# Stage buffers of a two-block network start 128 bytes past a multiple of 512

## The chip, the cores and the metric

The kernel runs on one core of one Trainium2 chip. The metric is the device time of one launch, in microseconds (us), from the runs' own times; the profile is one further execution, taken by the hardware profiler.

## The reference

Two blocks of a network are applied in turn to 256 tokens of width 1024, all in float32. Cut to what matters:

```python
def swiglu(x, w_gu, w_down):
    gate, up = jnp.split(x @ w_gu, 2, axis=-1)
    return (jax.nn.silu(gate) * up) @ w_down          # 1024 -> 2 x 2816 -> 1024

def first_block(x, ...):
    for l in range(2):
        if l == 1: k, v = shared_kv(h, kv_norm_g, w_kv)
        h = h + 0.5 * rmsnorm(swiglu(rmsnorm(h, g[0]), ffn_w_gu[l, 0], ffn_w_down[l, 0]), g[1])
        mix = short_gated_conv(...) if l == 0 else diff_attention(...)
        h = h + rmsnorm(mix, g[3])
        h = h + 0.5 * rmsnorm(swiglu(rmsnorm(h, g[4]), ffn_w_gu[l, 1], ffn_w_down[l, 1]), g[5])

def second_block(x, ...):
    proj = rmsnorm_2(x, attn_norm) @ w_in              # q, k, v, index, SSD and gate columns
    y_attn = dsa_attention(...)                        # sparse attention over 64 chosen keys
    y_ssd = gated_group_rmsnorm(ssd_chunked(...), z, ssd_norm)
    merged = sigmoid(gate_a) * (y_attn @ w_attn_branch) + sigmoid(gate_b) * (y_ssd @ w_ssd_branch)
    x = x + merged @ w_out
    return x + hier_moe(rmsnorm_2(x, ffn_norm), ...)   # 32 experts, 2 of them for each token
```

## The kernel before

The program is one long sequence for each engine, written by hand, with semaphores between the engines. All weights but the experts' come as a stream of slots of 1 MB (128 partitions by 2048 floats). SP's queue loads slot after slot into `raw`, a ring of 6, as soon as TensorE has done with the slot 6 places before. ScalarE rounds each slot to the one-pass format fp32r (`whi`, line 318), VectorE takes the rest (`wlo`, line 329, which lies over `raw`), and the activations are split the same way into a high and a low part. Each product is then three matmuls: high by high, high by low, low by high.

Nearly all matmuls of the stream are of one kind: the stationary operand is a 128x128 piece of a split activation, loaded anew for each matmul, and the moving operand is 256 or 512 columns of `whi` or `wlo`. In the names of the profile `Y<-whi,hh` means: into `Y`, moving `whi`, stationary `hh`. Line 431 (`half_columns`) is gate and up of the feed-forward, with the normed input `xh`, `xl` as the stationary operand; line 461 (`some_rows`) is every product by a slot of rows, among them the down product with `hh`, `hl`; line 400 (`row_slot`) is the attention branch's product with `ya_hi`, `ya_lo`.

A feed-forward has 11 steps, each of 48 matmuls of line 431, the transposes of 256 hidden columns for two token tiles (line 728, moving `ident` in `cst`, stationary `hf`), and 24 matmuls of line 461. There are four feed-forwards. The other row products with a buffer of their own are the convolution's (`ch`, `cl`, 96 matmuls), the attention branch (`ya_hi`, `ya_lo`, 96) and the SSD branch (`ys_hi`, `ys_lo`, 192). Key and value, the attention output and the last product of block two use `xh` and `xl`.

The experts' weights are not split: their matmuls are plain fp32, with 32 gathered rows (`xt_rows`, line 2992, and `ht`, line 3013) stationary and 1 MB pieces in 20 places moving: the ring `raw`, the ring `whi` (named `raw_whi` there), `xh` and `xl` (named `raw_x`), `xn`, and `far`. SP's queue loads a piece when its place is free, first as the last slots of the stream are done with.

Where a buffer starts is set by the order of allocation. `align` puts a filler ahead of the buffers of a stage:

```python
        def align(name, where=ctx):
            short = -nc.sbuf_base % LINE          # LINE = 128
            if short:
                sb(name, [P, short // 4], where=where)
```

Every piece of a split activation that is loaded as a stationary operand starts a multiple of 512 bytes behind its buffer's start, and so does every 512-column piece of a weight slot. So one number tells how they lie: the start of the buffer modulo 512, called its residue here. Worked out from the allocations:

```
buffer                                   residue before   after
raw, wlo, whi, h, xn, xh, xl, cst             128           128
far                                           480           480
gains, gs, hf, hh, hl (feed-forward)          256           128
ch, cl, u, ut, bs (convolution)               256           128
kt, vt, qt, ex, at, qs, ov, on (attention)    256           128
tok_ya, ya_hi, ya_lo, zs, ys_lo, dd           256           128
xs, ys_hi, bt, ct, cb, mm, cr, no, one        256           128
vv, k2, qt2 (sparse attention)                256           128
adm, score, sm2, ex2                            0           384
xt_rows, ht_2, hf_2, gs_2, sel2 (experts)      64           480
gx (gathered rows)                             96             0
```

The small buffers `ss`, `rs` and `rt` (64 columns each) hold sums of squares, inverse roots and scratch. GpSimd computes the roots with a power of -0.5 that stands in a column of `rt`.

Of the kernel before, what the change touches and what calls it, by code (L numbers as in the profile page):

```python
# [8 lines left out]
ALU = mybir.AluOpType  # L9
ACT = mybir.ActivationFunctionType  # L10
X = mybir.AxisListType.X

P = 128
T = 256
NT = T // P
# [11 lines left out]
TILES = EXPERTS + EXTRA  # L27
PAIRS = TILES // 2
ABSENT = 4096
LINE = 128  # L30
NOWHERE = 1 << 20
PLACES = 20
EPS = 1e-6
# [88 lines left out]
def build(nc, stream, experts, x_in, out, cols, const, attn_const, adm_const, rows, lam_in, nothing):  # L122
# [7 lines left out]
    with ctx:  # L130
        def sb(name, shape, dt=F32, where=ctx):
            return where.enter_context(nc.sbuf_tensor(name, shape, dt))

        def align(name, where=ctx):

            short = -nc.sbuf_base % LINE
            if short:
                sb(name, [P, short // 4], where=where)

        def signal(name, base=0):  # L140
            return Signal(ctx.enter_context(nc.semaphore(name)), base)

        def pair(name):
            return [signal(f"{name}{t}") for t in range(NT)]
# [13 lines left out]
        col = sb("col", [P, N_COLS])  # L158
        ss = sb("ss", [P, 64])
        rs = sb("rs", [P, 64])  # L160
        rt = sb("rt", [P, 64])
        dt_raw = sb("dt_raw", [P, NT, 32])
        ident = cst[:, C_ID:C_ID + P]

# [39 lines left out]
        rstd_ready = pair("rstd_ready")  # L204
        yr_ready = pair("yr_ready")
# [33 lines left out]
        scratch_set = signal("scratch_set")  # L239
# [36 lines left out]
        plink = Link(ctx.enter_context(nc.semaphore("pool_order")))  # L276
# [226 lines left out]
        def rstd_of(t):  # L503
            return rs[:, 52 + t:53 + t]
# [29 lines left out]
        def pool_post_root(pool, t):  # L534

            a, y = ss[:, 50 + t:51 + t], rs[:, 50 + t:51 + t]
            pool.wait_ge(ysq_done[t].sem, ysq_done[t].at(1))
            plink(pool, nc.gpsimd.tensor_scalar(a, ss[:, 54 + 2 * t:55 + 2 * t], ss[:, 55 + 2 * t:56 + 2 * t], EPS,  # L538
                                                ALU.add, ALU.add))
            nc.gpsimd.tensor_tensor(y, a, rt[:, 63:64], ALU.pow).then_inc(yr_ready[t].sem, 1)  # L540

        def pool_rstd(pool, t):
            pool.wait_ge(hsq_done[t].sem, hsq_done[t].at(0))
            a = rt[:, 52 + t:53 + t]
            plink(pool, nc.gpsimd.tensor_scalar(a, ss[:, 52 + t:53 + t], EPS, None, ALU.add))
            nc.gpsimd.tensor_tensor(rstd_of(t), a, rt[:, 63:64], ALU.pow).then_inc(rstd_ready[t].sem, 1)

        def load_gain(i, after):
            @block.gpsimd
# [768 lines left out]
        class DiffAttention:  # L1318
# [34 lines left out]
            def run(self, kt, vt, scores_in, leave, then):  # L1353
# [4 lines left out]
                nm, su, rc, oq, og = self.nm, self.su, self.rc, self.oq, self.og  # L1358
# [208 lines left out]
                @block.gpsimd  # L1567
                def _(pool):
                    for t in range(NT):
                        pool_rstd(pool, t)  # L1570
                    for u in range(self.UNITS):
                        a = oq[:, u % 2, :]
                        pool.wait_ge(osq_done.sem, osq_done.at(u))
                        if u >= 2:
                            pool.wait_ge(on_ready.sem, on_ready.at(u - 2))
                        plink(pool, nc.gpsimd.tensor_scalar(a, a, EPS, None, ALU.add))
                        nc.gpsimd.tensor_tensor(og[:, u % 2, :], a, rt[:, 63:64].broadcast_to([P, 2]), ALU.pow
                                                ).then_inc(or_ready.sem, 1)
                    for t in range(NT):
                        leave.pool(pool, t)  # L1580
# [96 lines left out]
        def sparse_attention(tok_, ya_hi, ya_lo, iw, zs, dd, dsk, entry):  # L1677
# [20 lines left out]
            @block.gpsimd  # L1698
            def _(pool):
                for t in range(NT):  # L1700
                    pool.wait_ge(new_h[t].sem, new_h[t].base)
                pool.dma_start(adm[:, :, :], adm_const.rearrange("p (t k) -> p t k", t=NT)
                               ).then_inc(phase_in[1].sem, 16)
                pool.dma_start(gr[:, :, :], rows["qk"].partition_broadcast(P)).then_inc(phase_in[1].sem, 16)
                pool.dma_start(dsk[:, :, :], rows["ssd"].partition_broadcast(P)).then_inc(ssd_in.sem, 16)
# [53 lines left out]
            @block.gpsimd  # L1759
            def _(pool):  # L1760
                pool.wait_ge(key_squared.sem, NT)
                plink(pool, nc.gpsimd.tensor_scalar(rt[:, 40:42], ss[:, 40:42], EPS, None, ALU.add))
                nc.gpsimd.tensor_tensor(rs[:, 40:42], rt[:, 40:42], rt[:, 63:64].broadcast_to([P, 2]), ALU.pow
                                        ).then_inc(key_root.sem, 1)

            @block.tensor
# [185 lines left out]
            @block.gpsimd  # L1952
            def _(pool):

                g = nc.gpsimd
                x, m, e, z, z2, p, dt, da = (dd[:, i] for i in range(8))
                by_tile = [a.rearrange("p (t h) -> p t h", t=NT) for a in (x, dt, da)]
                pool.wait_ge(act_free.sem, act_free.at(2))
                pool.wait_ge(ssd_in.sem, 16)
                plink(pool, g.tensor_tensor(by_tile[0], dt_raw[:, :, :], dsk[:, 0:1, :].broadcast_to([P, NT, 32]), ALU.add))  # L1960
                plink(pool, g.tensor_scalar(m, x, 0.0, None, ALU.max))
                plink(pool, g.tensor_scalar(p, m, 2.0, None, ALU.mult))
                g.tensor_tensor(p, p, x, ALU.subtract).then_inc(dt_in.sem, 1)
                pool.wait_ge(dt_exp.sem, 2)
                plink(pool, g.tensor_scalar(z, e, 2.0, None, ALU.add))
                plink(pool, g.tensor_tensor(z, z, rt[:, 62:63].broadcast_to([P, NT * 32]), ALU.pow))
                plink(pool, g.tensor_tensor(z, z, e, ALU.mult))
                plink(pool, g.tensor_tensor(z2, z, z, ALU.mult))
                plink(pool, g.tensor_scalar(p, z2, 1.0 / 15, None, ALU.mult))
                for q in (13, 11, 9, 7, 5, 3):  # L1970
                    plink(pool, g.tensor_scalar(p, p, 1.0 / q, None, ALU.add))
                    plink(pool, g.tensor_tensor(p, p, z2, ALU.mult))
                plink(pool, g.tensor_scalar(p, p, 1.0, 2.0, ALU.add, ALU.mult))
                plink(pool, g.tensor_tensor(p, p, z, ALU.mult))
                plink(pool, g.tensor_tensor(dt, p, m, ALU.add))
                plink(pool, g.tensor_tensor(by_tile[2], by_tile[1], dsk[:, 1:2, :].broadcast_to([P, NT, 32]), ALU.mult))
                plink(pool, g.tensor_scalar(da, da, -1.0, None, ALU.mult))

                da4 = dd[:, 2:6].rearrange("p a b -> p (a b)").rearrange("p (t r h) -> p t r h", t=NT, r=4)
                for t in range(NT):  # L1980
                    g.tensor_copy(da4[:, t], by_tile[2][:, t, :].unsqueeze(1).broadcast_to([P, 4, 32])).then_inc(da_ready.sem, 1)
# [283 lines left out]
        class StateSpace:  # L2265
# [347 lines left out]
            def pool_root(self, pool, g):  # L2613
                a = ss[:, 2 * g:2 * g + 2]
                pool.wait_ge(gated_sq.sem, 2 * g + 2)
                plink(pool, nc.gpsimd.tensor_scalar(a, a, EPS, None, ALU.add))
                nc.gpsimd.tensor_tensor(rs[:, 2 * g:2 * g + 2], a, rt[:, 63:64].broadcast_to([P, 2]), ALU.pow
                                        ).then_inc(gated_root.sem, 1)

        place_far = (nc.sbuf_top - 5 * 4 * SLOT) // 32 * 32  # L2620
# [551 lines left out]
        @block.scalar  # L3172
        def _(act):
            act.wait_ge(scratch_set.sem, 1)
            nc.scalar.activation(rt[:, 60:61], rt[:, 61:62], ACT.Silu)
            act.wait_ge(cols_in.sem, 16)

        @block.vector
# [7 lines left out]
        class NormedEntry:  # L3186
# [8 lines left out]
                                     accum_out=ss[:, 52 + t:53 + t]).then_inc(hsq_done[t].sem, 1)  # L3195

            def root(self, pool, t):
                a = rt[:, 52 + t:53 + t]
                plink(pool, nc.gpsimd.tensor_scalar(a, ss[:, 52 + t:53 + t], EPS, None, ALU.add))
                nc.gpsimd.tensor_tensor(rstd_of(t), a, rt[:, 63:64], ALU.pow).then_inc(rstd_ready[t].sem, 1)  # L3200

            def scale(self, t):
                for c in range(2):
# [48 lines left out]

        @block.gpsimd
        def _(pool):
            nc.gpsimd.memset(rt[:, 60:62], 0.0).then_inc(scratch_set.sem, 1)
            plink(pool, nc.gpsimd.memset(rt[:, 63:64], -0.5))
            plink(pool, nc.gpsimd.memset(rt[:, 62:63], -1.0))

        first = ExitStack()
        align("rest_first", first)  # L3260
        gains = sb("gains", [P, 2, D], where=first)
        bufs = ffn_buffers(first, "_1")
# [33 lines left out]

        with ExitStack() as mixer:
            align("rest_ya", mixer)
            place_ya = (nc.sbuf_base + 31) // 32 * 32
            tok_ya = sb("tok_ya", [P, 4096], where=mixer)  # L3300
# [200 lines left out]
```

## Time and profile before

| what | value |
|---|---|
| median of 3 runs | 1675.75 us (1674.76 to 1676.12) |
| the profiled execution's own time | 1676.05 us |
| its span, first to last instruction | 1674.2 us |
| PE (TensorE matmul) busy | 1550.8 us, 93% of the span |
| DVE (VectorE) busy | 915.2 us |
| ACT (ScalarE) busy | 761.8 us |
| POOL (GpSimd) busy | 152.1 us |
| mean granted TensorE clock | 0.974 of 2.4 GHz |

The span is cut into stages in the order of the reference: the feed-forwards lie at about 9 to 200, 310 to 490, 541 to 720 and 828 to 1010 us, block two's projections and SSD at 1010 to 1350, its output products up to 1414, and the experts from there to the end. Matmuls overlap in the records: one of 512 columns is shown as lasting about 390 ns, while the next one starts about 230 ns after it. How fast TensorE works is read from the starts.

### The profile page before, as it was taken

To read this page: it belongs to the slowest core of one execution; us is meant where nothing else is said; L and a number is where in the kernel's file an instruction comes from. 1 tells how busy PE (TensorE), PEld (TensorE's weight loads), DVE (VectorE), ACT (ScalarE), POOL (GpSimd) and SP (SyncE) were. 2 spreads that over 40 slices of the span, in tenths; PEclk is the share of its full clock that TensorE was granted. 3 is DMA by queue.
4 is the path that set the end of the run, shared out by engine and by line. 5 is a ranking of instruction groups with operands and counts; after the bars stand their busy time and mean duration, and the time that the engine had idled before them with its cause. 6 is when DMAs were issued, how large, how long until landed. Compare 5 with 4: busy or idle time off the path is not lost.

```text
span 1674.2 us, 23054 instructions
## 1 busy us (share of the span) xinstructions
PE 1550.8 (93%) x9664; PEld 1253.5 (75%) x9664; DVE 915.2 (55%) x1298; ACT 761.8 (46%) x1201; POOL 152.1 (9%) x202
## 2 busy tenths in 40 slices
PE   7999999999999999997999999999999999677676
PEld 6888888788887888876788878877989977333332
DVE  5545576744564544577745455786866765410102
ACT  6444554544455444466644444547655653111111
POOL 0000000100010000011100001050001000232330
PEclk9999999999999999999999999999999999798998
DMA  7555555545557455532355554432452258999996
GB/s 280 187 179 195 204 164 176 188 177 186 191 176 281 162 178 191 184 126 102 139 194 183 183 194 139 170 109 101 173 176 102 102 186 337 354 415 414 413 415 271
DMA packets 55366, 347.23 MB, mean 207 GB/s; under 512 B 10516, under 2 KB 10916, under 8 KB 15168
## 3 DMA queue, kind: packets, MB, share of 16 engines
q1 hardware_dynamic: 47520, 333.17, 54.0%
q0 software_dynamic: 7744, 12.61, 2.3%
q8 instruction: 76, 1.25, 0.3%
q14 instruction: 26, 0.21, 0.0%
HBM read 396.34 MB, written 9.96 MB: 243 GB/s over the span
## 4 chain that ended last, share of the span: by engine, by line
PE 77%; DVE 7%; DMA 7%; ACT 4%; issue 3%; POOL 1%; DVEq 0%; SPq 0%; POOLq 0%; ACTq 0%
PE A L431 31%; PE Y L461 20%; PE A L384 6%; PE A L369 4%; PE A L2992 3%; DMA raw<-experts,extra 3%; PE Y L3013 2%; DMA raw_whi<-experts 2%; DVE wlo L329 1%; PE A L445 1%; PE Y L400 1%; DMA raw<-stream 1%; ACT whi L318 1%; PE A L728 1%; DVE xn L528 1%
## 5 line engine op out<-in xcount | busy, mean ns | idle before, releaser
L329 DVE TENSOR_TENSOR wlo<-raw,whi 128x2048 fp32r<-128x2048 f32 (+1 forms) x226 | 496.8, 2205 | 243.9 <-ACT whi L318 243.1
L318 ACT ACTIVATE whi<-raw 128x2048 fp32r<-128x2048 f32 (+1 forms) x226 | 415.6, 1847 | 91.2 <-DMA raw<-stream 91.1
L431 PE MATMUL A<-whi,xh 128*128 128x512 f32 x768 | 309.0, 402 | 5.1 <-DVE wlo L329 5.1
L431 PE MATMUL A<-whi,xl 128*128 128x512 f32 x768 | 301.9, 393 | 0.0
L431 PE MATMUL A<-wlo,xh 128*128 128x512 f32 x768 | 301.0, 392 | 0.0
L431 PEld LDWEIGHTS A<-whi,xh 128*128 128x128 f32 x768 | 145.1, 189 | 33.9 <-DVE wlo L329 5.9
L431 PEld LDWEIGHTS A<-whi,xl 128*128 128x128 f32 x768 | 145.0, 189 | 31.8
L431 PEld LDWEIGHTS A<-wlo,xh 128*128 128x128 f32 x768 | 145.5, 189 | 28.5
L461 PE MATMUL Y<-whi,hh 128*128 128x512 f32 x352 | 140.5, 399 | 1.2 <-DVE hl L808 1.2
L461 PE MATMUL Y<-whi,hl 128*128 128x512 f32 x352 | 138.9, 395 | 0.0
L461 PE MATMUL Y<-wlo,hh 128*128 128x512 f32 x352 | 138.9, 395 | 0.0
L770 ACT ACTIVATE hh<-A 128x256 fp32r<-128x256 f32 x88 | 33.9, 385 | 202.2 <-PE A L728 202.2
L384 PE MATMUL A<-whi,xh 128*128 128x256 f32 (+1 forms) x400 | 118.3, 296 | 4.7 <-DVE wlo L329 2.6
L384 PE MATMUL A<-whi,xl 128*128 128x256 f32 (+1 forms) x400 | 114.2, 285 | 0.0
L384 PE MATMUL A<-wlo,xh 128*128 128x256 f32 (+1 forms) x400 | 114.1, 285 | 0.0
L766 ACT ACTIVATE gs<-A,rs 128x256 f32<-128x256 f32 x88 | 41.8, 475 | 135.8 <-PE A L431 135.8
L808 DVE TENSOR_TENSOR hl<-A,hh 128x256 fp32r<-128x256 f32 x88 | 37.0, 420 | 98.5 <-ACT hh L770 97.6
L538 POOL TENSOR_SCALAR ss<-ss 128x1 f32<-128x1 f32 x12 | 13.0, 1084 | 852.3 <-ACT xn L513 852.3
L3083 DVE TENSOR_TENSOR xt_rows<-A,col 128x512 f32<-128x512 f32 x24 | 16.6, 691 | 134.8 <-PE A L2982 134.8
L384 PEld LDWEIGHTS A<-whi,xh 128*128 128x128 f32 x400 | 77.7, 194 | 10.0 <-issue 7.6
L816 DVE SCALAR_TENSOR_TENSOR hf<-A,rs,gs 128x256 f32<-128x256 f32 x88 | 42.4, 482 | 69.6 <-ACT gs L766 69.5
L2992 PE MATMUL A<-far,xt_rows 128*32 128x256 f32 x432 | 53.4, 462 | 28.2 <-DMA raw<-experts,extra 24.8
(464 smaller groups left out, 2798.3 us busy)
## 6 DMA issues: line engine op xcount, KB each, us to landing
raw<-stream SPq DMA_DIRECT2D x216, 1024.0 KB, 4.8
raw_whi<-experts SPq DMA_DIRECT2D x39, 1024.0 KB, 28.5
raw<-experts SPq DMA_DIRECT2D x22, 1024.0 KB, 28.0
far<-experts SPq DMA_DIRECT2D x17, 1024.0 KB, 26.5
raw_x<-experts SPq DMA_DIRECT2D x12, 1024.0 KB, 28.9
xn<-experts SPq DMA_DIRECT2D x6, 1024.0 KB, 28.1
gains<-post_rows POOLq DMA_DIRECT2D x6, 512.0 KB, 5.2
far<-sums_at SPq DMA_DIRECT2D x4, 512.0 KB, 8.3
```

Of the source, the lines that this page charges most:

```text
L318: nc.scalar.activation(whi[:, n % RING, c], raw[:, n % RING, c], ACT.Copy).then_inc(hi_ready.sem, 1)
L329: nc.vector.tensor_tensor(wlo[:, n % RING, c], raw[:, n % RING, c], whi[:, n % RING, c].bitcast(F32), ALU.subtract).then_inc(lo_ready.sem, 1)
L369: ins = nc.tensor.matmul(bank[:, m, :], lhsT=lhs, rhs=rhs, start=(k == 0 and q == 0), stop=(k == KD - 1 and q == 2))
L384: ins = nc.tensor.matmul(bank[:, m, :], lhsT=lhs[:, k, tok(m)], rhs=w[:, k, 0:width], start=(k == 0 and q == 0), stop=(k == KD - 1 and q = ...
L431: ins = nc.tensor.matmul(bank, lhsT=lhs[:, kk, tok(t)], rhs=w[:, k, :], start=(kk == 0 and q == 0), stop=(kk == KD - 1 and q == 2))
L461: ins = nc.tensor.matmul(banks[c], lhsT=lhs[:, j, :], rhs=w[:, j, cc], start=(start and j == 0 and q == 0), stop=(stop and j == 1 and q == 2))
L766: nc.scalar.activation(gs[:, t, s % 2, :], bank(t, s)[:, 0:256], ACT.Silu, scale=rstd_of(t)).then_inc(gate_ready[t].sem, 1)
L770: nc.scalar.activation(hh[:, t, turns % 2], bank(t, turns)[:, 0:256].rearrange("p (j t) -> p j t", j=2), ACT.Copy).then_inc(hid_hi[t].sem, 1)
L808: v_.tensor_tensor(hl[:, t, s % 2], bank(t, s)[:, 0:256].rearrange("p (j t) -> p j t", j=2), hh[:, t, s % 2].bitcast(F32), ALU.subtract).t ...
L816: v_.scalar_tensor_tensor(hf[:, t, s % 2, :], bank(t, s)[:, 256:512], rstd_of(t), gs[:, t, s % 2, :], ALU.mult, ALU.mult).then_inc(hid_rea ...
L2992: ins = nc.tensor.matmul(gate_up(q)[group(c, j), :], lhsT=xt[:, q % 2, k, group(part, j)], rhs=w[j][:, k, c, :], start=(part == 0 and k == 0),
L3013: ins = nc.tensor.matmul(down_bank(q)[group(c, j), :], lhsT=ht[:, q % 2, group(f, j)], rhs=w[j][:, f, c, :], start=f == 0, stop=f == 1)
```

## The change

The filler of `align` now brings the next buffer to 128 modulo 512 bytes, where before it brought it to a multiple of 128. `rt` is cut from 64 to 40 columns, and the columns of it that GpSimd and one warm-up activation used move to free columns of `ss`. No buffer before `dt_raw` moves, and the residues of all others are in the table above. The instructions of every engine, their order, their shapes and their waits are the same as before; a few read or write `ss` where they had `rt`.

```diff
-LINE = 128
+LINE, LINE_START = 512, 128
...
         def align(name, where=ctx):
 
-            short = -nc.sbuf_base % LINE
+            short = (LINE_START - (nc.sbuf_base + 31) // 32 * 32) % LINE
             if short:
                 sb(name, [P, short // 4], where=where)
...
-        rt = sb("rt", [P, 64])
+        rt = sb("rt", [P, 40])
...
         def pool_rstd(pool, t):
             pool.wait_ge(hsq_done[t].sem, hsq_done[t].at(0))
-            a = rt[:, 52 + t:53 + t]
+            a = ss[:, 58 + t:59 + t]
             plink(pool, nc.gpsimd.tensor_scalar(a, ss[:, 52 + t:53 + t], EPS, None, ALU.add))
-            nc.gpsimd.tensor_tensor(rstd_of(t), a, rt[:, 63:64], ALU.pow).then_inc(rstd_ready[t].sem, 1)
+            nc.gpsimd.tensor_tensor(rstd_of(t), a, ss[:, 63:64], ALU.pow).then_inc(rstd_ready[t].sem, 1)
...
-            nc.gpsimd.memset(rt[:, 60:62], 0.0).then_inc(scratch_set.sem, 1)
-            plink(pool, nc.gpsimd.memset(rt[:, 63:64], -0.5))
-            plink(pool, nc.gpsimd.memset(rt[:, 62:63], -1.0))
+            nc.gpsimd.memset(ss[:, 60:62], 0.0).then_inc(scratch_set.sem, 1)
+            plink(pool, nc.gpsimd.memset(ss[:, 63:64], -0.5))
+            plink(pool, nc.gpsimd.memset(ss[:, 62:63], -1.0))
```

## Rows read from the trace of the kernel before

**Rows 1.** The page: span, and busy time of each engine.
```profile
span 1674.2 us, 23054 instructions
...
PE 1550.8 (93%) x9664; PEld 1253.5 (75%) x9664; DVE 915.2 (55%) x1298; ACT 761.8 (46%) x1201; POOL 152.1 (9%) x202
```

**Rows 2.** Windows 60-200, 320-495, 550-720, 840-1000 us, in the feed-forwards: their sum.
```profile
sum 645.00, PE 644.59 PEld 525.76 DVE 328.10 ACT 283.62 POOL 7.21; mean PE 161.15 PEld 131.44 DVE 82.02 ACT 70.90 POOL 1.80
```

**Rows 3.** The chain that ended last, one step of a feed-forward: start, us, what.
```profile
75.91 5.48 PE A L431 x24
81.38 5.59 PE Y L461 x24
```

**Rows 4.** Groups on PE: busy us, mean ns of one; out<-moving,stationary.
```profile
L461 PE MATMUL Y<-whi,hh 128*128 128x512 f32 x352 | 140.5, 399 | 1.2 <-DVE hl L808 1.2
...
L461 PE MATMUL Y<-whi,ys_hi 128*128 128x512 f32 x64 | 25.6, 400 | 1.5 <-DVE wlo L329 1.5
...
L461 PE MATMUL Y<-whi,ch 128*128 128x512 f32 x32 | 13.0, 407 | 0.7 <-DVE cl L1113 0.7
...
L400 PE MATMUL Y<-whi,ya_hi 128*128 128x512 f32 x32 | 10.1, 397 | 0.0
```

**Rows 5.** Timeline of PE: starts with a stationary operand at residue 128.
```profile
60.14 0.39 PE L431 MATMUL A<-whi,xh 128*128 128x512 f32 x1
...
63.99 0.40 PE L431 MATMUL A<-whi,xl 128*128 128x512 f32 x1
...
523.92 0.39 PE L461 MATMUL Y<-whi,xl 128*128 128x512 f32 x1
...
532.08 0.39 PE L461 MATMUL Y<-whi,xl 128*128 128x512 f32 x1
```

**Rows 6.** Timeline of PE: starts with a stationary operand at residue 256.
```profile
64.23 0.40 PE L461 MATMUL Y<-whi,hh 128*128 128x512 f32 x1
...
69.58 0.40 PE L461 MATMUL Y<-whi,hl 128*128 128x512 f32 x1
...
1233.29 0.62 PE L400 MATMUL Y<-whi,ya_lo 128*128 128x512 f32 x2
...
1254.21 0.62 PE L400 MATMUL Y<-whi,ya_lo 128*128 128x512 f32 x2
...
1367.21 0.40 PE L461 MATMUL Y<-whi,ys_hi 128*128 128x512 f32 x1
...
1372.81 0.40 PE L461 MATMUL Y<-whi,ys_hi 128*128 128x512 f32 x1
```

**Rows 7.** Timeline of PE: residue 128 behind residue 256, and behind transposes.
```profile
355.88 0.39 PE L431 MATMUL A<-whi,xh 128*128 128x512 f32 x1
...
358.39 0.39 PE L431 MATMUL A<-whi,xl 128*128 128x512 f32 x1
...
538.39 0.39 PE L461 MATMUL Y<-wlo,xh 128*128 128x512 f32 x1
...
540.70 0.39 PE L461 MATMUL Y<-whi,xl 128*128 128x512 f32 x1
```

**Rows 8.** Tile xt_rows: the expert stage's fp32 matmuls, ns min/median/max.
```profile
L2992 PE MATMUL A<-raw,xt_rows x480: 379/379/636, 1448.5 to 1649.7; 128*32 128x256 f32 x160
...
L2992 PE MATMUL A<-far,xt_rows x432: 376/379/636, 1441.8 to 1656.0; 128*32 128x256 f32 x144
```

**Rows 9.** Windows of the end: us, PE, PEld, DVE, ACT, POOL, PEclk, DMA share, GB/s.
```profile
1441.00:1551.00 110.00, 88.83 (x1084) 44.29 (x1088) 16.12 (x36) 15.64 (x37) 32.51 (x32) 0.89 0.98 391
1551.00:1650.00 99.00, 67.83 (x823) 32.98 (x815) 9.38 (x18) 12.11 (x30) 26.53 (x27) 0.90 1.00 408
```

**Rows 10.** The chain around the start of the expert stage.
```profile
1350.26 36.71 PE Y L461 x156
...
1459.43 10.88 DMA raw<-experts,extra
```

**Rows 11.** Timeline of SP's queue: expert loads wait for stream slots.
```profile
1390.65 1.28 SPq L2666 DMA_DIRECT2D far<-experts  x3
```

More of the change, by code:

```diff
@@ L539, in pool_post_root @@
                                                 ALU.add, ALU.add))
-            nc.gpsimd.tensor_tensor(y, a, rt[:, 63:64], ALU.pow).then_inc(yr_ready[t].sem, 1)
+            nc.gpsimd.tensor_tensor(y, a, ss[:, 63:64], ALU.pow).then_inc(yr_ready[t].sem, 1)
         def pool_rstd(pool, t):
             pool.wait_ge(hsq_done[t].sem, hsq_done[t].at(0))
-            a = rt[:, 52 + t:53 + t]
+            a = ss[:, 58 + t:59 + t]
             plink(pool, nc.gpsimd.tensor_scalar(a, ss[:, 52 + t:53 + t], EPS, None, ALU.add))
-            nc.gpsimd.tensor_tensor(rstd_of(t), a, rt[:, 63:64], ALU.pow).then_inc(rstd_ready[t].sem, 1)
+            nc.gpsimd.tensor_tensor(rstd_of(t), a, ss[:, 63:64], ALU.pow).then_inc(rstd_ready[t].sem, 1)
         def load_gain(i, after):
@@ L1576, in _ @@
                         plink(pool, nc.gpsimd.tensor_scalar(a, a, EPS, None, ALU.add))
-                        nc.gpsimd.tensor_tensor(og[:, u % 2, :], a, rt[:, 63:64].broadcast_to([P, 2]), ALU.pow
+                        nc.gpsimd.tensor_tensor(og[:, u % 2, :], a, ss[:, 63:64].broadcast_to([P, 2]), ALU.pow
                                                 ).then_inc(or_ready.sem, 1)
@@ L1761, in _ @@
                 pool.wait_ge(key_squared.sem, NT)
-                plink(pool, nc.gpsimd.tensor_scalar(rt[:, 40:42], ss[:, 40:42], EPS, None, ALU.add))
-                nc.gpsimd.tensor_tensor(rs[:, 40:42], rt[:, 40:42], rt[:, 63:64].broadcast_to([P, 2]), ALU.pow
+                plink(pool, nc.gpsimd.tensor_scalar(ss[:, 44:46], ss[:, 40:42], EPS, None, ALU.add))
+                nc.gpsimd.tensor_tensor(rs[:, 40:42], ss[:, 44:46], ss[:, 63:64].broadcast_to([P, 2]), ALU.pow
                                         ).then_inc(key_root.sem, 1)
@@ L1965, in _ @@
                 plink(pool, g.tensor_scalar(z, e, 2.0, None, ALU.add))
-                plink(pool, g.tensor_tensor(z, z, rt[:, 62:63].broadcast_to([P, NT * 32]), ALU.pow))
+                plink(pool, g.tensor_tensor(z, z, ss[:, 62:63].broadcast_to([P, NT * 32]), ALU.pow))
                 plink(pool, g.tensor_tensor(z, z, e, ALU.mult))
@@ L2616, in pool_root @@
                 plink(pool, nc.gpsimd.tensor_scalar(a, a, EPS, None, ALU.add))
-                nc.gpsimd.tensor_tensor(rs[:, 2 * g:2 * g + 2], a, rt[:, 63:64].broadcast_to([P, 2]), ALU.pow
+                nc.gpsimd.tensor_tensor(rs[:, 2 * g:2 * g + 2], a, ss[:, 63:64].broadcast_to([P, 2]), ALU.pow
                                         ).then_inc(gated_root.sem, 1)
@@ L3174, in _ @@
             act.wait_ge(scratch_set.sem, 1)
-            nc.scalar.activation(rt[:, 60:61], rt[:, 61:62], ACT.Silu)
+            nc.scalar.activation(ss[:, 60:61], ss[:, 61:62], ACT.Silu)
             act.wait_ge(cols_in.sem, 16)
@@ L3197, in root @@
             def root(self, pool, t):
-                a = rt[:, 52 + t:53 + t]
+                a = ss[:, 58 + t:59 + t]
                 plink(pool, nc.gpsimd.tensor_scalar(a, ss[:, 52 + t:53 + t], EPS, None, ALU.add))
-                nc.gpsimd.tensor_tensor(rstd_of(t), a, rt[:, 63:64], ALU.pow).then_inc(rstd_ready[t].sem, 1)
+                nc.gpsimd.tensor_tensor(rstd_of(t), a, ss[:, 63:64], ALU.pow).then_inc(rstd_ready[t].sem, 1)
             def scale(self, t):
```

## The prediction

> **What bounds the kernel now.** The page comes first: PE is busy for 1550.8 of 1674.2 us, DVE and ACT for 915 and 762 [rows 1]. Then the windows, since a share over the whole span says little: in four stretches inside the feed-forwards, 645 us together, PE is busy for 644.6 us [rows 2]. No other engine comes near, so a nanosecond off a matmul there is a nanosecond off the time. The chain of waits agrees: one step of a feed-forward is a chain of PE pieces alone [rows 3].
>
> A busy PE is not a fast PE, because matmuls overlap in the records. The mean durations of the groups, some 400 ns, can't be added up [rows 4]. What counts is the distance from one start to the next. I looked at it for one shape, 512 columns moving, a fresh 128x128 stationary piece for each matmul, moving operand always in `whi` or `wlo` (residue 128). The reader is to compare two groups:
>
> - Stationary piece at residue 128. Line 431 with `xh`, `xl` starts at 60.14 and, 17 starts later, at 63.99 us: 226.5 ns each. Line 461 with `xh`, `xl` (key and value) goes from 523.92 to 532.08 us in 36 starts: 226.7 ns [rows 5].
> - Stationary piece at residue 256. Line 461 with `hh`, `hl` goes from 64.23 to 69.58 us in 23 starts: 232.6 ns. Line 400 with `ya_hi`, `ya_lo` needs 20.92 us for 90 starts: 232.4 ns. Line 461 with `ys_hi`, `ys_lo` needs 5.60 us for 24: 233.3 ns [rows 6].
>
> So one line of code, 461, runs at 226.7 or at 232.6 ns by which buffer is stationary. The layout inside the buffer doesn't explain it: `ya_hi` and `ys_hi` are laid out as `xh` is, pieces 1024 bytes apart, and are as slow as `hh`, whose pieces are 512 bytes apart. Nor do the neighbours: the two stretches at 60 to 70 us stand in the same feed-forward, one right behind the other. What is left is where the buffer lies, and the residue is the part of that which all the buffers at 232 to 233 ns share.
>
> **The change part by part.**
>
> *Row products with a stage buffer.* `hh`, `hl`, `ch`, `cl`, `ya` and `ys` go from residue 256 to 128, where `xh` is. Their number: three passes each of 352 with `hh`, 64 with `ys_hi`, 32 with `ch` and 32 with `ya_hi` [rows 4], so 3 x 480 = 1440 matmuls. Each is to lose 232.6 - 226.7 = 5.9 ns [rows 5, 6]. 1440 x 5.9 ns = 8.5 us. The bounds: 0 if place above some address is the cause and not the residue; for the other end, the fastest pace of rows 5 against the slowest of rows 6, 6.8 ns, 9.8 us.
>
> *What follows them.* A block of line 431 behind a block with `hh` opens slower than it goes on: 11 starts in 2.51 us, 228.2 ns, from 355.88 us [rows 7]. Against 226.7 that is 16 ns for a block, and 48 such blocks stand in the timeline: 0.8 us. I take it, because a block at one residue throughout should have nothing to settle. The bounds are 0 and 0.8.
>
> *What the transposes leave.* Behind a group of transposes the pace is 231.0 ns for ten starts, 2.31 us from 538.39 us, although both operands of the matmuls are at residue 128, and the transposed `h` and `cst` too [rows 7]. That is 43 ns lost for each block behind transposes, and the change doesn't touch its cause. Twenty of the blocks to be sped up open that way (counted in the timeline), so some 0.8 us of the 8.5 stay. For the 76 blocks of line 431 behind the transposes of `hf`, which does go from 256 to 128, I take nothing, because `h` at 128 shows the same loss; if all of it went, 76 x 0.043 = 3.3 us would be the outer bound.
>
> *Pairs that move together.* `kt` with `qt`, `vt` with `at`, `ct` with `bt`, `no` with `one`, `xs` with `mm` had 256 on both sides and get 128 on both. All are few. Together with matmuls of stream slots by `xh` (lines 384, 369, 445, 431), where neither side moves, they get nothing.
>
> *The expert stage.* `xt_rows` and `ht` go from 64 to 480. These are plain fp32 matmuls, and here the trace has a control as well: with `xt_rows` at 64 as the stationary operand, `raw` moving (128) shows a median of 379 ns and `far` moving (480) the same 379 [rows 8]. The residue of one operand against the other's is not seen in them. What covers a small loss: from 1441 to 1650 us PE is busy for 88.8 + 67.8 = 156.7 of 209 us, while the DMA engines are at 0.98 and 1.00 [rows 9]. I cost it at nothing. Without that cover, the 5.9 ns on 1920 such records (1536 of line 2992, 384 of line 3013) would be 11 us (rows 8 show 912 of the 1920, the groups of the same two lines the others). The few fp32 matmuls of the sparse attention, whose `ex2` goes from 0 to 384, are costed in the same way.
>
> *The scratch columns.* The roots on POOL keep their number, shape and waits; they read a neighbouring buffer. Nothing.
>
> *Does the gain reach the end?* The stage behind is bound by transfers [rows 9], so one must ask what starts them. SP's queue issues the expert loads as slots of the stream come free, in bulk from 1390.65 us on [rows 11], and the slots are freed by line 461, which is the chain there [rows 10]. What TensorE saves up to that point moves the transfers forward by as much. Nearly all of the 1440 matmuls lie before it. The chain then runs on such loads as the one at 1459.43 us [rows 10], 10.88 us, whose length the change leaves alone.
>
> **The sum.** 8.5 + 0.8 - 0.8 = 8.5 us. The profiled execution's own time is 1676.05 us, 1.85 above its span and 0.3 above the median; 1676.05 - 8.5 = 1667.55, and by the median 1675.75 - 8.5 = 1667.2 us, which I give.
>
> **The rivals.**
>
> *No change (1675.8 us).* The stage buffers all lie above byte 153,000, and `xh` and `xl` end at 147,584, so place rather than residue could be it. For it speaks that no buffer in the trace tells the two apart. Against it: `whi` at 65,664 and `xh` at 131,200 are far apart and work together at 226.7 ns, and the stage buffers, which start anywhere from 153,344 to 197,376, all show 232 to 233. A limit between 147,584 and 153,344 would be a coincidence.
>
> A rule of the Trainium skill comes to the same time. The Trainium skill, SBUF — State Buffer, section "Who interferes with whom", says that PE has two read ports, one for the moving operand and one for the weights, and that "PE and ACT never wait on anyone". By that rule placing one operand against the other gives nothing, and the time would stay at 1675.8 us. The rows do not agree with it as it stands: 226.7 against 232.6 ns for one line of code.
>
> *Part of it (1671 us).* The residue matters, but 128 on both sides is only good for pieces 1024 bytes apart, as in `xh`; `hh`, whose pieces are 512 apart, stays slow. Then only the 384 matmuls of `ch`, `ya` and `ys` gain, 2.3 us, to 1673.5; with half of the effect on `hh` as well, 3.1 us more, 1670.4. For it: no row shows 512-byte pieces at 128. Against it: at 256 the two spacings are equally slow.
>
> *Slower (over 1679 us).* The expert stage, with `xt_rows` and `ht` at 480, could slow down until TensorE and not the transfers bound it. PE has 209 - 156.7 = 52.3 us free there [rows 9], so the loss must pass 52.3 / 1920 = 27 ns for each record before it shows, and 52.3 + 8.5 + 3.4 = 64.2 us, 33 ns each, before the whole is slower by 0.2%. At 35 ns it would be 1675.75 - 8.5 + (67.2 - 52.3) = 1682. Rows 8 show 0 for a residue that differs.
>
> **How the numbers follow.** The full effect has 0.73 and lies between 1665.5 (9.8 us by the outer pace, some of it kept by the transposes) and 1669.5. Part of it: 0.12, up to 1673.5. More than the sum, by the 3.3 us of the `hf` transposes: 0.02. No change: 0.09. Slower: 0.04. A measurement of this kernel tells a difference from none at about 0.2%, 3.4 us, that is below 1672.4. The upper piece of the partial case, some 0.02, falls on the side of no change: faster 0.85, same 0.11, slower 0.04. The range takes in the full effect and most of the partial one, 1664.5 to 1673, and holds about 0.86; its lower end allows for a part of the transposes' loss.
>
> **What the next profile would show.** Line 461 with `hh` would start every 226.7 ns and a block of 24 in the chain would be 5.59 - 0.14 = 5.45 us. Lines 400 and 461 with `ya` and `ys` would show the same. The block of line 431 behind it would open at 226.7. Line 431 behind `hf` transposes would still open slow. The DMA-bound stretch would start some 8 us earlier and last as long. The prediction is wrong if the `hh` pace stays at 232.6 (place, or spacing), or if it falls and the end doesn't move (the transfers did not follow, or the expert stage gave it back).

## The result and the profile after

The changed kernel runs in 1666.55 us (median of 6 runs, 1664.21 to 1668.05), the kernel before in 1675.93 us (6 runs, 1670.84 to 1679.15). The ratio is 0.9945 with a 95% interval of 0.9929 to 0.9961, so 9.2 us less, between 6.5 and 11.9. 1667.2 us had been forecast.

The profiled execution took 1668.05 us, its span is 1666.1. The page shows it, with PE busy for 10.6 us less than in [rows 1] and DVE, ACT and POOL as before:

```profile
span 1666.1 us, 23054 instructions
...
PE 1540.2 (92%) x9664; PEld 1251.9 (75%) x9664; DVE 915.7 (55%) x1298; ACT 762.9 (46%) x1201; POOL 152.4 (9%) x202
```

Inside the four feed-forwards, moved along with the stages, PE is as full as in [rows 2]; the sum of the windows 60-200, 320-490, 550-715 and 840-995 us is

```profile
sum 630.00, PE 629.09 PEld 517.77 DVE 323.40 ACT 281.99 POOL 7.45; mean PE 157.27 PEld 129.44 DVE 80.85 ACT 70.50 POOL 1.86
```

The chain answers to [rows 3] and [rows 10]. Its columns are start, length, and what:

```profile
74.77 5.47 PE A L431 x24
80.24 5.44 PE Y L461 x24
```

```profile
1225.79 21.85 PE Y L400 x96
```

The block of 24 of line 461 takes 5.44 us where it took 5.59, and line 400's 96 matmuls take 21.85 us (the same block of before, 1232.45 us, took 22.38). The router's product, line 874, stands ahead of the experts. In the chain of before and of after:

```profile
1414.36 1.71 PE A L874 x16
```

```profile
1406.91 1.71 PE A L874 x16
```

It starts 7.45 us earlier.

The starts, read as in [rows 5 to 7]:

```profile
63.25 0.39 PE L461 MATMUL Y<-whi,hh 128*128 128x512 f32 x1
...
68.47 0.39 PE L461 MATMUL Y<-whi,hl 128*128 128x512 f32 x1
68.69 0.39 PE L431 MATMUL A<-whi,xh 128*128 128x512 f32 x1
```

```profile
352.73 0.39 PE L431 MATMUL A<-whi,xh 128*128 128x512 f32 x1
...
355.22 0.39 PE L431 MATMUL A<-whi,xl 128*128 128x512 f32 x1
...
355.90 0.39 PE L431 MATMUL A<-wlo,xh 128*128 128x512 f32 x1
...
358.19 0.39 PE L431 MATMUL A<-whi,xl 128*128 128x512 f32 x1
```

From 63.25 to 68.47 us there are 23 starts of line 461 with `hh`, `hl`, 5.22 us, 227.0 ns each, against 232.6 in [rows 6]. The block of line 431 behind `hh` opens at (355.22 - 352.73) / 11 = 226.4 ns, against 228.2 in [rows 7]. Behind the transposes of `hf` it is (358.19 - 355.90) / 10 = 229.0 ns: not settled, yet better than before. The same ten starts in the kernel before took (361.38 - 359.07) / 10 = 231.0 ns:

```profile
359.07 0.40 PE L431 MATMUL A<-wlo,xh 128*128 128x512 f32 x1
...
361.38 0.39 PE L431 MATMUL A<-whi,xl 128*128 128x512 f32 x1
```

At the end of the program the fp32 matmuls are as in [rows 8], with `xt_rows` now at 480, and the windows are as in [rows 9], 8 us earlier. The expert loads start at 1383.14 us where [rows 11] has 1390.65:

```profile
L2992 PE MATMUL A<-raw,xt_rows x480: 379/379/636, 1440.7 to 1644.4; 128*32 128x256 f32 x160
...
L2992 PE MATMUL A<-far,xt_rows x432: 376/379/636, 1434.3 to 1650.7; 128*32 128x256 f32 x144
```

```profile
1433.00:1543.00 110.00, 87.08 (x1086) 43.54 (x1088) 16.21 (x36) 15.65 (x37) 32.55 (x32) 0.91 0.98 393
1543.00:1642.00 99.00, 67.60 (x782) 32.25 (x778) 9.39 (x18) 11.53 (x29) 25.88 (x26) 0.84 1.00 407
```

```profile
1383.14 1.28 SPq L2666 DMA_DIRECT2D far<-experts  x3
```

### The profile page after: what moved, and what is told of

Read it like the earlier page. It is cut to its first block, busy times and chain, and to the rows that moved or that the text cites. A ratio compares the mean times of both kernels' runs of the same rounds, so it can differ in the third digit from the quotient of the medians.

```text
span 1666.1 us, 23054 instructions
## 1 busy us (share of the span) xinstructions
PE 1540.2 (92%) x9664; PEld 1251.9 (75%) x9664; DVE 915.7 (55%) x1298; ACT 762.9 (46%) x1201; POOL 152.4 (9%) x202
## 4 chain that ended last, share of the span: by engine, by line
PE 75%; DMA 9%; DVE 8%; ACT 4%; issue 3%; POOL 1%; SPq 0%; DVEq 0%; POOLq 0%; ACTq 0%
PE A L431 31%; PE Y L461 20%; PE A L384 6%; DMA raw_whi<-experts 5%; PE A L369 4%; PE A L2992 3%; DVE wlo L329 2%; DMA raw<-experts,extra 2%; PE Y L3013 2%; PE A L445 1%; PE Y L400 1%; ACT whi L318 1%; DMA raw<-stream 1%; PE A L728 1%; PE Y L564 1%
```

## The experiments

Theory 1 was that the residue of the stationary operand against the moving one sets the pace. The rivals were that 128 is a good residue by itself, that the place in the memory counts and not the residue, and that the folded scratch columns or the experts' buffers brought the gain.

**Back to 256, the fold kept.**

```diff
-LINE, LINE_START = 512, 128
+LINE, LINE_START = 512, 256
```

> The changed kernel with the stage buffers put back to residue 256; the scratch columns stay folded together and the experts' buffers stay where the change put them (xt_rows at 480). Theory 1 (what counts is the residue of the stationary operand against the moving one): line 461 with hh, and lines 400 and 461 with ya and ys, start every 232 to 233 ns again, a chain block of 24 is 5.59 us, and the time is that of the kernel before, ratio 1.000. Theory 2 (128 is a good residue for a stationary operand by itself): the same. Rival (the folded scratch columns or the experts' buffers brought the gain): the time stays at that of the changed kernel, ratio 0.9945.

Measured: 1674.99 us, ratio 0.9992 (0.9981 to 1.0003). Chain rows for lines 461 and 400:

```profile
63.91 5.59 PE Y L461 x24
```

```profile
1234.15 22.38 PE Y L400 x96
```

Both blocks are back at their old lengths, so the fold and the experts' buffers brought nothing that could be measured.

**All large buffers at 256.**

```diff
-LINE, LINE_START = 512, 128
+LINE, LINE_START = 512, 256
...
+        sb("lead", [P, 32])
         place = (nc.sbuf_base + 31) // 32 * 32
         raw = sb("raw", [P, RING, SLOT])
```

> The changed kernel with every large buffer moved up by 128 bytes: the weight ring, h, xn, xh, xl, cst and the stage buffers all at residue 256. Theory 1 (residue against residue): nothing differs from the changed kernel, starts every 226.7 ns everywhere, ratio 0.9945. Theory 2 (128 by itself is good for a stationary operand): xh and xl are slow too, 232.6 ns for all 4128 one-pass matmuls of 512 columns, that is 1440 x 5.9 = 8.5 us lost against the changed kernel and some 12 us more on xh and xl, ratio about 1.007. A limit by place: hh, ya and ys slow, xh not, ratio 1.000.

Measured: 1663.1 us, ratio 0.993 (0.9906 to 0.9954). Lines are one higher in this kernel (462 is 461, 401 is 400):

```profile
62.70 5.44 PE Y L462 x24
```

```profile
1222.33 21.86 PE Y L401 x96
```

Here `ya_hi` and `hh` lie at the very bytes where they lay in the kernel before, and are at full pace. So neither 128 by itself nor the place is the cause: that rival falls. What counts is the distance between the two operands, which is the same here as in the changed kernel. (The time holds a second effect, of the transfers; it is told at the last experiment.)

**The weight ring at 128, all others at 256.**

```diff
-LINE, LINE_START = 512, 128
+LINE, LINE_START = 512, 256
...
+        sb("lead", [P, 32])
         h = sb("h", [P, NT, D])
```

> The changed kernel with the weight ring left at residue 128 and h, xn, xh, xl, cst and the stage buffers at 256. Theory 1: all 4128 one-pass matmuls of 512 columns have their operands 128 bytes apart in residue and start every 232 to 233 ns, line 431 with xh among them. Against the kernel before that is 2688 more at 5.9 ns, 15.9 us, less the 3 us or so that the blocks behind transposes lose there already: ratio about 1.007. What matmuls of 256 columns do (lines 384, 369, 445, now some 120 ns from start to start) no row has shown; if they lose as much, 2300 x 5.9 = 13.6 us more, ratio 1.016. Theory 2: the same for line 431. A limit by place: line 431 keeps 226.7 ns and the time is that of the kernel before, ratio 1.000.

Measured: 1680.89 us, ratio 1.0034 (1.0021 to 1.0047). The direction is that of theory 1, the size is less than half. Line 431 is slow too, 432 here:

```profile
73.42 2.80 PE A L432 x12
...
76.43 5.58 PE A L432 x24
82.01 5.58 PE Y L462 x24
```

```profile
1188.81 5.70 PE A L370 x48
```

Its block of 24 takes 5.58 us, 232.5 ns each, against 5.48 us, 228.3 ns, in [rows 3]. My working took 226.7 ns as the pace that would be lost; but the blocks of line 431 between transposes never ran at that, and 4.2 ns was what they had to lose. A step of a feed-forward lost 0.10 us there and 0.09 in its other two blocks (2.78 and 2.80 against 2.74 and 2.75), 8.4 us for 44 steps. Over the whole program, when every PE start is set against the same one of the kernel before (how is told under *The count* below), lines 431 and 461 with `xh`, `xl` lost 9.9 us, where 15.9 less 3 had been expected. And matmuls of 256 columns don't lose: 48 of line 369 (370 here) take 5.70 us where the kernel before has 5.76, and all of them together gained 1.5 us. Line 874 (875 here) starts at 1420.36 us, 6.0 us later than before.

**Only the feed-forward's buffers at 128.**

```diff
         bufs = ffn_buffers(first, "_1")
+        sb("between", [P, 32], where=first)
...
-            align("rest_ya", mixer)
+            align("rest_ya", mixer, 256)
...
-            align("rest_iw", mixer)
+            align("rest_iw", mixer, 256)
```

(`align` takes the residue as an argument there.)

> The changed kernel with only the feed-forward's buffers (gains, gs, hf, hh, hl) at residue 128; the convolution's, the attention's and block two's are at 256 again. All theories of residue: line 461 with hh starts every 226.7 ns, with ch and ys every 232 to 233 ns, line 400 with ya likewise. 384 of the 1440 matmuls are slow again, 384 x 5.9 = 2.3 us, and so the profiled span is some 2.3 us above that of the changed kernel, ratio about 0.996. If the effects did not add up by count, the span would be off this by more than the 3 us that runs differ by.

Measured: 1665.27 us, ratio 0.9933 (0.9912 to 0.9955).

```profile
63.10 5.44 PE Y L461 x24
```

```profile
1225.48 22.38 PE Y L400 x96
```

The two blocks are independent of each other, as forecast. The 2.3 us can't be seen in the whole time: the span, 1665.5 us, is 0.6 below the changed kernel's, and profiles of one kernel differ by more than that (below). They can be seen in the starts: with `ch`, `ya` and `ys` 1.9 us of the changed kernel's gain are gone, and 0.6 us come back with other matmuls of these stages.

**The distance varied.** To make room, `dt_raw` is allocated among block two's buffers, and `LINE_START` is 64, 192, 0, 384, 96 or 160. The first of them as a diff:

```diff
-LINE, LINE_START = 512, 128
+LINE, LINE_START = 512, 64
...
-        dt_raw = sb("dt_raw", [P, NT, 32])
...
-            iw = sb("iw", [P, NT, IDX_HEADS], where=mixer)
+            iw, dt_raw = sb("iw", [P, NT, IDX_HEADS], where=mixer), sb("dt_raw", [P, NT, 32], where=mixer)
```

> The changed kernel with the stage buffers at residue 64, so 64 bytes below the weight ring's 128 (dt_raw is allocated with block two's buffers, to make room). Theory A (only equal residues settle at 226.7 ns, any distance costs the same beat): hh, ya, ys start every 232 to 233 ns. Theory B (the cost grows with the distance): about half of the 5.9 ns, some 229.5 ns. Theory C (64 bytes stand within one unit of the memory): 226.7 ns. Line 431 with xh keeps 226.7 where it is settled.

> The same with the stage buffers at residue 192, 64 bytes above the weight ring's. Theory A: 232 to 233 ns. Theory B: some 229.5 ns, as at 64. Theory C: 226.7 ns.

> The same with the stage buffers at residue 0, 128 bytes below the weight ring's. If the distance counts whatever its sign, 232 to 233 ns for hh, ya and ys, as 128 bytes above gave; if starting at a multiple of 512 is good in itself, 226.7 or less.

> The same with the stage buffers at residue 384, 256 bytes from the weight ring's, the farthest there is modulo 512. Theory A: 232 to 233 ns. Theory B: more than at 128 bytes, up to 238 ns, and the span some 8 us above that of the kernel before. A period of 256 bytes and not of 512: 226.7 ns, as with equal residues.

> The stage buffers at residue 96, 32 bytes below the weight ring's. Measured so far, by the distance of the stationary from the moving operand modulo 256: 0 gives 226.7 to 227.1 ns, -64 gives 229.0, 64 gives 233.3, 128 gives 232.5. If the curve is smooth below zero, 227 to 229 ns for hh, ya and ys. A pace below 226.7 would mean that equal residues are not the best.

> The stage buffers at residue 160, 32 bytes above the weight ring's. By the same curve, between 227 (distance 0) and 233.3 ns (64): some 230 ns. If any distance above zero costs the whole, 233 ns.

Single executions of these took 1671.17, 1675.69, 1673.52, 1666.14, 1672.76 and 1677.36 us. The clean reading is the block of line 400 in the chain, 96 matmuls without a break; for 64, 192, 0, 384, 96 and 160, one fence for each:

```profile
1229.61 22.07 PE Y L400 x96
```

```profile
1233.69 22.48 PE Y L400 x96
```

```profile
1232.31 22.38 PE Y L400 x96
```

```profile
1225.29 21.85 PE Y L400 x96
```

```profile
1229.99 22.48 PE Y L400 x96
```

```profile
1235.09 22.48 PE Y L400 x96
```

With the weight ring at 128, and the block divided by 96 (it ends with the last matmul's own length, so this is a little above the distance of the starts):

| stationary at | distance | block, us | ns each |
|---|---|---|---|
| 128 | 0 | 21.85 | 227.6 |
| 384 | 256 | 21.85 | 227.6 |
| 64 | -64 | 22.07 | 229.9 |
| 0 | -128 | 22.38 | 233.1 |
| 256 | 128 | 22.38 | 233.1 |
| 96 | -32 | 22.48 | 234.2 |
| 160 | 32 | 22.48 | 234.2 |
| 192 | 64 | 22.48 | 234.2 |

384 is as good as 128, and -128 is like 128. The period is therefore 256 bytes; the change asked for more than was needed. None of the theories on the distance held: a step of 32 bytes costs the whole, -64 costs a third of that, and 64 bytes up is not like 64 bytes down. No distance that was tried is better than none. All distances but 0 were tried with the weight ring at 128 alone, so that they cost the same with the ring elsewhere is not shown.

**The changed kernel once more, beside all at 256.**

> The changed kernel once more, beside the next one on the same chip. Ratio 0.9945 as before. It also tells how far one profile lies from another: the first 512-column matmuls of the stages should come within 1 or 2 us of the first profile's.

> All large buffers at residue 256, as in the second experiment, where it was at 0.993 with an interval that touches the changed kernel's. Theory 1, refined by the experiment at 384 to residues modulo 256: only the distance between the operands counts, so the ratio is the changed kernel's, 0.9945, and the 3.5 us between the two were spread. If 256 for all is really better, the ratio stays at 0.993 or below and the paces must show where, which they did not.

Measured side by side on one chip: the changed kernel 1665.99 us, ratio 0.9934 (0.992 to 0.9948); all at 256, 1665.39 us, ratio 0.993 (0.9917 to 0.9943). They can't be told apart in time, and no version beats the changed kernel beyond doubt. The two profiles of all at 256 differ by 5.8 us in span (1659.1 and 1664.9), and the clock is part of it. The windows 500-520 and 520-540 us of the second profile and of the first (us, PE, PEld, DVE, ACT, POOL, PEclk, DMA share, GB/s):

```profile
500.00:520.00 20.00, 16.93 (x78) 13.81 (x77) 5.28 (x4) 5.45 (x5) 0.00 (x0) 0.96 0.99 363
520.00:540.00 20.00, 20.00 (x86) 16.42 (x86) 7.97 (x9) 11.71 (x19) 0.00 (x0) 0.87 0.43 155
```

```profile
500.00:520.00 20.00, 17.77 (x83) 14.45 (x82) 6.26 (x3) 7.26 (x9) 0.00 (x0) 1.00 0.96 369
520.00:540.00 20.00, 20.00 (x98) 16.72 (x97) 9.90 (x13) 13.10 (x18) 0.00 (x0) 1.00 0.59 212
```

In the second profile PE waits longer for the slots of key and value, and the granted clock falls to 0.87 as the mean of the 20 us behind it: the same 42 matmuls of line 462 take 12.64 us there and 9.82 in the first.

The end of the program does differ with all at 256. From line 874 (875 there) to the end it is 255.7 us in both of its profiles, and 257.4 to 259.8 in the twelve profiles of the other versions. The transfers are faster. From 1500 to 1600 us of the changed kernel, of this one, and of the third experiment (columns as in [rows 9]):

```profile
1500.00:1600.00 100.00, 72.74 (x862) 35.92 (x866) 10.23 (x20) 12.00 (x30) 26.10 (x26) 0.88 1.02 415
```

```profile
1500.00:1600.00 100.00, 73.94 (x866) 36.99 (x870) 10.41 (x20) 11.99 (x30) 28.29 (x29) 0.88 1.02 421
```

```profile
1500.00:1600.00 100.00, 70.79 (x854) 34.34 (x850) 10.43 (x20) 11.98 (x30) 27.64 (x28) 0.88 1.02 415
```

Both profiles with all at 256 show 421 GB/s, the twelve others 414 or 415. Of the 20 places that the experts are loaded into, 15 start at 256 modulo 512 here (`raw`, `whi`, `xh`, `xl`, `xn`); in the third experiment the 12 of the two rings stay at 128, and the rate with them. So where a transfer's destination starts costs some 1.5% where transfers bound the stage, a second effect of placing, apart from the first. No experiment moved the rings alone.

## Why the prediction was right

*The pace.* This step held: 226.7 ns was forecast for `hh`, 227.0 was read, and a block of 24 came to 5.44 us where 5.45 had been forecast. The reason given held too: the experiment with all buffers at 256 shows that the distance of the two operands counts, which the prediction could only argue from the buffers' places. The residue had to be taken modulo 256, though, not 512. For 256 against 128 both say the same, so the error cost nothing.

*The count.* The two programs issue the same 9664 PE instructions in the same order. So each distance from one start to the next can be set against the same one of the kernel before, and the differences added up by buffer, up to line 874; what differs by more than 60 ns (a wait, or another clock) is left aside. In the two profiles of the changed kernel the gain by this working is, in us:

| stationary | first | second | forecast |
|---|---|---|---|
| `hh`, `hl` | 5.85 | 5.83 | |
| `ch`, `ya`, `ys` and their low parts | 1.98 | 2.00 | |
| these together | 7.8 | 7.8 | 8.5 - 0.8 |
| line 431 behind `hh` | 0.60 | 0.60 | 0.8 |
| line 431 behind transposes of `hf` | 0.99 | 1.00 | 0 |
| all others | -0.6 | -0.6 | 0 |
| sum | 8.8 | 8.85 | 8.5 |

The 0.8 us taken off for blocks that open behind transposes were right: without them the first term would have been 0.7 us too large.

*The settling behind `hh`.* 0.8 us was forecast, 0.6 came, for 45 such blocks where 48 had been counted. In the second feed-forward the first block of 12 behind line 461, and the next one, which stands behind transposes of `hf`, are in the chain before and after:

```profile
356.04 2.74 PE A L431 x12
...
359.00 2.77 PE A L431 x12
```

```profile
352.89 2.72 PE A L431 x12
...
355.83 2.75 PE A L431 x12
```

The first of the two went from 2.74 to 2.72 us.

*The transposes of `hf`.* I took nothing, because `h` at 128 shows the same loss. That term was mis-sized: it came to 1.0 us for 76 blocks, inside the outer bound of 3.3. The ten starts shown above went from 231.0 to 229.0 ns, the median of the 76 blocks from 231.3 to 229.2. A part of the loss behind these transposes did go with the residue, and a part stayed. The size is good to some 0.3 us: in the two profiles with all at 256 it is 0.65 and 1.01, and in two at the old distance, where it should be 0, -0.3 and 0.1.

*What was put at nothing.* The other matmuls lost 0.6 us, half of it line 384's. With the convolution's, the attention's and block two's buffers back at 256, in the fourth experiment, they lost none. Which pair does it was not looked for. This and the transposes of `hf` are two errors of opposite sign in the sum; that they nearly cancel is luck.

*The way to the end.* Up to line 874 the lead over the kernel before, by which PE starts the same instruction earlier, came to 7.45 us in the first profile and 8.6 in the second, not 8.8: waits and the clock take the rest, and they differ from one execution to the next. The largest piece is in the sparse attention, where the lead falls from 8.0 us to 6.5, and from 9.1 to 7.6 in the second profile. The same 48 matmuls of line 384 in the chain, before and after, and the windows ahead of them and over them, before and after (columns as in [rows 9]):

```profile
1087.08 6.00 PE A L384 x48
```

```profile
1079.06 7.49 PE A L384 x48
```

```profile
1082.40:1087.40 5.00, 2.44 (x21) 2.27 (x20) 4.66 (x12) 2.81 (x5) 0.47 (x1) 1.00 0.44 149
1087.40:1092.40 5.00, 5.00 (x44) 5.00 (x43) 4.83 (x11) 1.25 (x1) 4.92 (x2) 1.00 0.26 107
```

```profile
1074.40:1079.40 5.00, 2.41 (x21) 2.24 (x20) 4.66 (x12) 2.86 (x5) 0.51 (x1) 1.00 0.44 138
1079.40:1084.40 5.00, 5.00 (x32) 5.00 (x31) 4.83 (x11) 1.21 (x1) 4.92 (x2) 0.66 0.27 111
```

PE is busy for 2.41 of the 5 us ahead; then the granted clock is 0.66 as a mean over 5 us, a mix of the levels 1.2 and 2.4 GHz. The kernel before, with 2.44 of 5 us ahead, kept 2.4 GHz there. Its own low clock comes later, in

```profile
1105.00:1110.00 5.00, 4.98 (x28) 4.30 (x29) 3.98 (x7) 2.14 (x9) 4.42 (x8) 0.66 0.00 0
```

By 1109 us the lead is back at 8.1 us, but by 1120 it is at 6.8: the changed kernel's chain runs over DVE and ACT there, so PE waits for them and the lead goes again. The low clock behind the idle stretch isn't the change: the experiment with all at 256 has 6.01 us for these 48 in its first profile and 7.50 in its second. The Trainium skill, TensorE: Matmul & The Clock Gate, section "Part 1: The HAM clock gate (the "warmup" mystery)", has the clock follow what PE did shortly before, in windows that run free of the program, so that equal programs can differ; that is in keeping with these rows.

*The experts.* From line 874 to the end it took 1674.2 - 1414.36 = 259.8 us before and 1666.1 - 1406.91 = 259.2 after. The transfer-bound stage moved forward as a whole, and `xt_rows` at 480 cost nothing that could be seen.

*The rivals.* "No change" by place fell with the experiment with all at 256. The Trainium skill, SBUF — State Buffer, section "Who interferes with whom", gives PE two independent read ports and says that PE never waits on anyone; from that alone the placing would give nothing. It leaves out what was measured here: with the place of one operand changed and nothing else, a matmul differs by 5.5 to 5.9 ns. The partial case, that 512-byte spacing would stay slow, fell with `hh` at 227.0 ns. The slower case needed 33 ns for each expert matmul; the median stayed at 379.

That the median of the runs, 1666.55 us, came within 0.7 us of the forecast is in part luck, since the measured gain is known only to between 6.5 and 11.9 us. What the profiles bear out is the sum of the terms.

What I got wrong in between is the size in the third experiment, told there. What remains open: what in the chip makes the distance count (the runs show that it does, not how), why distances of 32 and 64 bytes cost what they do (only positions in steps of 32 bytes, and only this pair of shapes, were tried), why a block behind fp32 transposes needs some ten matmuls to come to its pace, and why the expert stage, 3 us shorter with all buffers at 256, does not show in the whole time beyond the scatter of the runs.

## What to carry to other kernels

Where one-pass matmuls with a fresh stationary operand each set the time, compare the distance from start to start between lines of the same shape. If it differs by a few ns, look where the two operands start: here equal residues modulo 256 bytes were worth 5.9 of 232.6 ns, for a filler of at most 255 bytes. It is a matter of the pair, so a buffer that was once aligned loses this when the other one moves. Measure it by blocks of the chain that no transpose interrupts, which here repeat to 0.01 us from profile to profile, or by setting two programs with the same instructions against each other start by start, and not by the whole time, which here differs by several us from run to run. A control that moves everything together, as all at 256, tells a distance from a place; but look at what else moves with it, here the destinations of the transfers.

## What the runs showed of the hardware

- The pace of fp32r matmuls of 512 columns, with a new 128x128 stationary operand for each, depends on the distance of the operands' start addresses modulo 256: 21.85 us for 96 at 0, 22.07 at -64, 22.38 at 128, 22.48 at -32, 32 and 64.
- Matmuls of 256 columns don't lose by it: 48 of line 369 took 5.76 us at distance 0 and 5.70 at 128. The plain fp32 matmuls of the experts don't show it: a median of 379 ns with `xt_rows` at 64 and at 480.
- With 15 of the experts' 20 places starting at 256 modulo 512 bytes the bound stage's transfers ran at 421 GB/s, and at 414 or 415 with the rings at 128.
- One idle stretch of PE of 2.6 us in the sparse attention is followed by a granted clock of 0.66 over the next 5 us in some executions of one and the same kernel and not in others; it costs 1.5 us there.
